# Attention probabilities turned by VectorE block transposes and DMA instead of TensorE transposes

## The reference, cut to what matters

```python
h = x @ w_in[l] + b_in[l]              # q, k, v, z_a, u_g, v_g, z_g, g_a, g_g
scores = q k^T / 8 - slope * dist      # 8 heads of 64, 2 key heads, blocks of 128 queries,
                                       # each over its own and the previous block of 128 keys
m = max(scores.max(-1), sink)
p = exp(scores - m);  p = p / (p.sum(-1) + exp(sink - m))
y_a = (p @ v) * silu(z_a)
merged = sigmoid(g_a) * (y_a @ w_branch_attn) + sigmoid(g_g) * (y_g @ w_branch_gmlp)
x = layer_norm(ALPHA * x + merged @ w_out + b_out)
```

## Time and profile before

| | us |
|---|---|
| median of 3 runs | 1548.91 (1548.21 to 1549.33) |
| profiled execution, its own time | 1549.3 |
| its span in the profile | 1547.5 |
| TensorE busy | 1536.1 |
| VectorE busy | 1012.6 |
| ScalarE busy | 593.4 |
| GpSimd busy | 361.9 |

### The profile page before, as it was taken

The page is one execution under the profiler, slowest core; times in us unless marked ns, Lnnn a source line. Parts: engine busy times, 40 slices in busy tenths (PEclk is TensorE's granted clock), DMA queues, the critical chain, the costliest instruction groups (busy, mean ns, idle before and its releaser), DMA issues.

```text
span 1547.5 us, 29869 instructions
## 1 busy us (share of the span) xinstructions
PE 1536.1 (99%) x12455; PEld 1378.0 (89%) x12455; DVE 1012.6 (65%) x1686; ACT 593.4 (38%) x1070; POOL 361.9 (23%) x333
## 2 busy tenths in 40 slices
PE   9999999999999999999999999999999999999998
PEld 9999999999998899899998898888888988888887
DVE  6656565775867678586786676567516776576346
ACT  5323232253444344334444446482112346641121
POOL 0000000020422224042242124334530043343510
PEclk9999999999999999999999999999999999999999
DMA  5322322323342423424234143223224322222331
GB/s 170 110 82 89 103 83 82 110 82 109 91 131 78 117 91 111 118 76 124 85 98 152 55 135 101 73 72 102 89 82 149 117 83 82 82 82 82 117 128 55
DMA packets 130226, 153.97 MB, mean 99 GB/s; under 512 B 5196, under 2 KB 104944, under 8 KB 130096
## 3 DMA queue, kind: packets, MB, share of 16 engines
q1 hardware_dynamic: 119728, 138.71, 29.2%
q10 hardware_dynamic: 10288, 13.18, 2.5%
q0 software_dynamic: 80, 0.20, 0.1%
HBM read 143.43 MB, written 8.65 MB: 98 GB/s over the span
## 4 chain that ended last, share of the span: by engine, by line
PE 51%; DVE 1%; issue 0%
PE acc L410 14%; PE acc L412 14%; PE acc L411 14%; PE aux L412 1%; PE aux L411 1%; PE aux L410 1%; PE aux L1410 1%; PE aux L1440 1%; PE aux L1429 1%; PE aux L1430 0%; PE aux L1464 0%; PE aux L1377 0%; PE aux L638 0%; PE aux L640 0%; PE aux L571 0%; PE acc L1328 0%
## 5 line engine op out<-in xcount | busy, mean ns | idle before, releaser
L410 PE MATMUL acc<-xhis,whi 128*128 128x264 f32 (+2 forms) x1848 | 610.9, 331 | 0.0
L412 PE MATMUL acc<-xhis,wlo 128*128 128x264 f32 (+2 forms) x1848 | 602.2, 326 | 0.0
L411 PE MATMUL acc<-xlos,whi 128*128 128x264 f32 (+2 forms) x1848 | 601.8, 326 | 0.0
L412 PEld LDWEIGHTS acc<-xhis,wlo 128*128 128x128 f32 x1848 | 347.8, 188 | 29.3
L410 PEld LDWEIGHTS acc<-xhis,whi 128*128 128x128 f32 x1848 | 348.0, 188 | 28.9 <-issue 0.3
L411 PEld LDWEIGHTS acc<-xlos,whi 128*128 128x128 f32 x1848 | 348.2, 188 | 27.0
L405 POOL TENSOR_TENSOR wlo<-raw,whi 128x1024 fp32r<-128x1024 f32 x84 | 207.8, 2475 | 376.9 <-DVE whi L2591 376.9
L401 ACT ACTIVATE whi<-raw 128x1024 fp32r<-128x1024 f32 x158 | 164.0, 1048 | 132.4 <-PE acc L412 119.3
L405 DVE TENSOR_TENSOR wlo<-raw,whi 128x1024 fp32r<-128x1024 f32 x81 | 99.8, 1236 | 38.0 <-ACT whi L401 37.8
L2286 DVE TENSOR_TENSOR wlo<-raw,whi 128x1024 fp32r<-128x1024 f32 x77 | 95.0, 1236 | 27.3 <-ACT whi L401 27.1
L2591 DVE CAST whi<-raw 128x1024 fp32r<-128x1024 f32 x84 | 66.8, 797 | 54.0 <-PE acc L412 53.8
(11 more groups left out here) (392 smaller groups left out, 2784.8 us busy)
## 6 DMA issues: line engine op xcount, KB each, us to landing
raw<-in_w_in SPq DMA_DIRECT2D x38, 1024.0 KB, 5.3
raw<-in_hgrn_w_in SPq DMA_DIRECT2D x32, 1024.0 KB, 5.8
raw<-in_pool_w_in SPq DMA_DIRECT2D x15, 1024.0 KB, 5.6
raw<-in_pool_w_out SPq DMA_DIRECT2D x8, 1024.0 KB, 5.1
raw<-in_hgrn_w_out SPq DMA_DIRECT2D x8, 1024.0 KB, 5.1
raw<-in_w_out SPq DMA_DIRECT2D x8, 1024.0 KB, 5.1
v_turn<-vb ACTq DMA_DIRECT2D x8, 544.0 KB, 2.7
raw<-in_pool_w_grp SPq DMA_DIRECT2D x4, 1024.0 KB, 5.3
```

Source lines behind the costliest of these rows:

```text
L410: pe.matmul(dst, stat[0], mov[0], start=first, stop=False)
L411: pe.matmul(dst, stat[0], mov[1], start=False, stop=False)
L412: return pe.matmul(dst, stat[1], mov[0], start=False, stop=last)
```

## The change

Each scaled probability tile is transposed in blocks of 32x32 by VectorE (`dve.transpose`, two a step, on the probability of s-1, after the maximum) into one of three tiles `pb`. ScalarE writes the tile to `p_turn` in device memory in step s+2 (one DMA of 256 KB, 2 KB a row) and, for two probabilities at once, reads it back in four DMAs of 128 KB (runs of 512 bytes) into `pt`, which puts the blocks in their places. The reads are issued in the steps of `BACK_AT`. The value products run at the steps of `VALUES_AT` and wait for the reads (`pt_landed`). The transposes on TensorE and the copies on ScalarE are gone. In a step ScalarE issues the reads, then computes exp, then issues the write. Values and spatial weights are turned in step 6. The gated values use one buffer in place of two. The last value products come in step 19, one later than before.

```diff
+        pb = [rows[:, 0:SEQ].rearrange("p (b n j) -> p b n j", b=4, n=4) for rows in (sq[1], xn[1], kf)]
+        VALUES_AT = {10: 0, 14: 1, 17: 2, 19: 3}
+        BACK_AT = {4: 0, 6: 1, 10: 2, 11: 3, 14: 4, 15: 5, 17: 6, 18: 7}
+        p_turn = nc.dram_tensor("p_turn", (32, len(ATT), 4, SEQ), F32).ap()
...
 # att_tensor
-                for t in range(s - 6, s - 2) if s >= 6 and s % 4 == 2 else ():
+                for t in range(4 * VALUES_AT[s], 4 * VALUES_AT[s] + 4) if s in VALUES_AT else ():
-                    pe.wait_ge(apt_ready, 1 + base + t + 1)
+                    if b == 0:
+                        pe.wait_ge(pt_landed, 32 * (base + t + 4))
-                                           pt[t % 4][:, 2 * x + kb_, :],
+                                           pt[t % 4][:, :, 2 * x + kb_, :],
...
-                    for x in range(2):
-                        for kb_ in range(0 if b else 1, 2):
-                            mm = pe.transpose(aux2[:, 0, P * (2 * x + kb_):P * (2 * x + kb_ + 1)],
-                                              pr[t % 2][:, x, P * kb_:P * kb_ + P], ident[:, :])
...
 # att_scalar
-                    act.wait_ge(apt_full, base + t + 1)
...
-                    act.activation(pt[t % 4][:, :, :].rearrange("p (x k) q -> p x k q", x=2)[:, :, first:, :],
-                                   aux2[:, 0, :].rearrange("p (x k q) -> p x k q", x=2, k=2)[:, :, first:, :],
-                                   ACT.Copy).then_inc(apt_ready, 1)
+                if between is not None:
+                    between()
+                if 2 <= s < len(ATT) + 2:
+                    n = base + s - 2
+                    act.wait_ge(pb_ready, 2 * n + 2)
+                if s in BACK_AT:
+                    t = 2 * BACK_AT[s]
+                    for n in (base + t, base + t + 1):
+                        act.wait_ge(pb_sent[n % 3], 16 * (n // 3) + 16)
...
+                    if base + t >= 4:
+                        act.wait_ge(ao_full, base + 4 * (t // 4))
+                    for b in range(4):
+                        act.dma_start(pt_pairs[t // 2 % 2][32 * b:32 * b + 32, :, :, :, :].rearrange("p t a n j -> p (t a) (n j)"),
+                                      p_turn[:, t:t + 2, :, P * b:P * b + P].rearrange("p t a n -> p (t a) n")).then_inc(pt_landed, 16)
                 if s < len(ATT):
...
+                if 2 <= s < len(ATT) + 2:
+                    n = base + s - 2
+                    act.dma_start(p_turn[:, s - 2, :, :].rearrange("p a n -> a p n"),
+                                  pb[n % 3].rearrange("p b n j -> p (b n j)")).then_inc(pb_sent[n % 3], 16)
...
 # att_vector, behind the maximum of s
+                if 1 <= s < len(ATT) + 1:
+                    t = s - 1
+                    first, z = (0 if ATT[t][1] else 1), t % 2
+                    dve.wait_ge(aprob, 3 * (base + t) + 3)
+                    n = base + t
+                    if n >= 3:
+                        dve.wait_ge(pb_sent[n % 3], 16 * (n // 3))
+                    for x in range(2):
+                        dve.transpose(pb[n % 3][:, :, 2 * x + first:2 * x + 2, :].rearrange("p b k j -> p k b j"),
+                                      pr[z][:, x, P * first:2 * P].rearrange("p (k b j) -> p k b j", b=4, j=32))\
+                           .then_inc(pb_ready, 1)
```

More of the change, by code:

```diff
@@ L270, in program @@
                 brow = sb("brow", [P, D], where=in_rows)
-            pt_more = [sb(f"pt{s}", [P, 4, P], where=before_g) for s in (2, 3)]
+            pt_second = sb("pt_second", [P, 2, 4, 4, 32], where=before_g)
         gac = sb("gac", [P, 4, SEQ], where=in_c)
@@ L290, in program @@
             pr = [sb(f"pr{s}", [P, 2, 2 * P + 1], where=before_m) for s in range(2)]
-            pt = [sb(f"pt{s}", [P, 4, P], where=before_m) for s in range(2)] + pt_more
+            pt_first = sb("pt_first", [P, 2, 4, 4, 32], where=before_m)
+            pt_pairs = [pt_first, pt_second]
+            pt = [pt_pairs[t // 2][:, t % 2, :, :, :] for t in range(4)]
             sgc = [xn[0][:, 0:SEQ], rstd[:, 0:SEQ]]
@@ L355, in program @@
         aexp, aprob, sink_ready = sem("aexp"), sem("aprob"), sem("sink_ready")
-        apt_full, apt_ready, ao_full = sem("apt_full"), sem("apt_ready"), sem("ao_full")
+        pb_ready, pb_sent = sem("pb_ready"), [sem(f"pb_sent{n}") for n in range(3)]
+        pt_landed = sem("pt_landed")
+        ao_full = sem("ao_full")
         ya_ready, yahi_ready, yalo_ready = sem("ya_ready"), sem("yahi_ready"), sem("yalo_ready")
@@ L865, in c_slots @@
                     if stage == "za" and index == 0:
-                        side.append(("vtc", 0))
-                        side.append(("ws", 0))
+                        pass
                     elif att < len(ATT) and stage in ("za", "u", "vg", "zg", "ga", "gg"):
                         side.append(("att", att))
+                        if att == 6:
+                            side += [("vtc", 0), ("ws", 0)]
                         att += 1
-                    elif att < len(ATT) + 3 and att >= len(ATT):
+                    elif att <= max(VALUES_AT) and att >= len(ATT):
                         side.append(("att", att))
@@ L1419, in att_tensor @@
                         pe.wait_ge(kc_low, 4 * i + 4)
-                        pe.wait_ge(ws_ready, i + 1)
                     if b == 0:
@@ L1431, in att_tensor @@
                     mm.then_inc(asc_full, 1)
[L1432 to L1437, removed]
-                    for x in range(2):
-                        for kb_ in range(0 if b else 1, 2):
-                            mm = pe.transpose(aux2[:, 0, P * (2 * x + kb_):P * (2 * x + kb_ + 1)],
-                                              pr[t % 2][:, x, P * kb_:P * kb_ + P], ident[:, :])
-                    mm.then_inc(apt_full, 1)
             def side_tensor(i, what, n):
@@ L1455, in side_tensor @@
                 elif what == "att":
-                    if n == 0:
+                    if n == min(VALUES_AT):
                         pe.wait_ge(vtc_ready, i + 1)
+                        pe.wait_ge(ws_ready, i + 1)
                     att_tensor(i, n)
@@ L1589, in _ @@
         def _(act):
-            act.sem_inc(apt_ready, 1)
             act.sem_inc(on_ready, 1)
@@ L1871, in att_scalar @@
                 base = 16 * i
+                if between is not None:
+                    between()
                 if 2 <= s < len(ATT) + 2:
-                    t = s - 2
-                    z, first = t % 2, (0 if ATT[t][1] else 1)
-                    act.wait_ge(apt_full, base + t + 1)
-                    if t >= 4:
-                        act.wait_ge(ao_full, base + t - 3)
+                    n = base + s - 2
[4 more added lines that the diff above has]
+                        act.wait_ge(pb_sent[n % 3], 16 * (n // 3) + 16)
                     if t == 2:
                         act.wait_ge(res_ready, 4 * i + 4)
-                    act.activation(pt[t % 4][:, :, :].rearrange("p (x k) q -> p x k q", x=2)[:, :, first:, :],
-                                   aux2[:, 0, :].rearrange("p (x k q) -> p x k q", x=2, k=2)[:, :, first:, :],
-                                   ACT.Copy).then_inc(apt_ready, 1)
-                if between is not None:
-                    between()
+                    if base + t >= 4:
[3 more added lines that the diff above has]
+                                      p_turn[:, t:t + 2, :, P * b:P * b + P].rearrange("p t a n -> p (t a) n")).then_inc(pt_landed, 16)
                 if s < len(ATT):
@@ L1887, in att_scalar @@
                     act.wait_ge(arow, base + s + 1)
+                    if i and s < 2:
+                        act.wait_ge(pb_ready, 2 * (base + s - 1))
                     for x in range(2):
@@ L1891, in att_scalar @@
                            .then_inc(aexp, 1)
-                if s >= 3 and ATT[s - 3][1] == CH - 1:
-                    p = ATT[s - 3][0]
+                if 2 <= s < len(ATT) + 2:
+                    n = base + s - 2
+                    act.dma_start(p_turn[:, s - 2, :, :].rearrange("p a n -> a p n"),
+                                  pb[n % 3].rearrange("p b n j -> p (b n j)")).then_inc(pb_sent[n % 3], 16)
+                if s in VALUES_AT:
+                    p = VALUES_AT[s]
                     act.wait_ge(ya_ready, 1 + 4 * i + p + 1)
-                    act.activation(yah[:, p, :], sq[p % 2][:, 0:SEQ], ACT.Copy).then_inc(yahi_ready, 1)
+                    act.activation(yah[:, p, :], sq[0][:, 0:SEQ], ACT.Copy).then_inc(yahi_ready, 1)
             for i in range(DEPTH):
@@ L2513, in att_vector @@
                     if b < 2:
+                        if s == 0:
+                            dve.wait_ge(c_landed, 32)
+                            dve.wait_ge(lc_landed, 96 * i + 96)
                         dve.tensor_copy(sc[z][:, :, 2 * P:2 * P + 1], sinks[:, 2 * p:2 * p + 2].unsqueeze(2))\
@@ L2523, in att_vector @@
```

(17 more changed lines are left out.)

## The result

The changed kernel is slower: 1565.66 us median (1564.73 to 1566.97, 4 runs) against 1548.81 (1548.21 to 1549.33, 4 runs), a ratio of 1.0108 with a 95% interval of 1.0096 to 1.0120. The forecast was 1541, the range 1535.5 to 1548, and the chance given to slower 0.10. Both forecast and range were wrong.

What follows compares the result with a forecast made beforehand. TensorE was taken as the bound, busy 1536.1 of 1547.5 us. Removed transposes -12.3, ScalarE's ring +1.0 and waits for turned probabilities +3.0 gave -8.3 us, a forecast of 1541, range 1535.5 to 1548.

Steps and rivals of the forecast that it cites:

- Removed transposes: TensorE, attention steps: 112 transposes gone, four cost 0.44 us and two 0.22 by score-product spacing, 12.3 us saved.
- Moving operand in runs of 32: TensorE's value products: reading probabilities as four runs of 32 columns per row brings no cost, nor gain.
- VectorE's block transposes: VectorE, after the maximum: 64 added, some 0.7 us a step and 20 us in all, hidden, cost 0.
- DMA issues: ScalarE's queue: 32 writes at 0.4 us and 64 reads at 0.37 us, 0.63 as the reads' other end.
- Rival (c): ScalarE's queue held by DMA issues averaging 1.0 us beside weight loads: +10.7 us, 1560; chance 0.10.
- The ring in zg: ScalarE's sigmoid-to-sigmoid turn, steps 11 to 14: 6.03 to 6.43 us; TensorE waits 0.5 a layer, +1.0 in all.
- The new wait: TensorE waits for turned probabilities before value products, chiefly at step 19: 1.5 us a layer, +3.0 in all.
- the wait at step 19: TensorE before the last value products, waiting for reads issued in step 18: 0 to 3.2 us.
- TensorE idling before a weight piece: Sign of a wrong mechanism: TensorE idles most elsewhere than forecast, such as step 10 or 14 or a weight piece.
- rival (a): All added work hidden: reads meet no weight load and ScalarE's ring keeps its slack; -12.3 us, 1537; chance 0.27.

Runs made afterwards that it cites:

- e4: The kernel before without 104 of its 112 probability transposes on TensorE, so the value products read what the buffers hold; 1537.45 us.
- e6: The changed kernel with only p_turn's dimension order altered, so a write is 128 rows instead of 4 blocks of 32 rows; 1538.64 us.
- e7: The changed kernel with p_turn laid out for writes of 128 rows and each write issued first in its step; 1537.81 us.
- e1: The changed kernel with its last value products at step 21 instead of 19 and the last two probabilities in their own tile; 1551.91 us.
- e5: The changed kernel with each step's write issued at its start, ahead of reads and exp, instead of behind exp; 1542.19 us.

## Why the prediction was wrong, point by point

- **Removed transposes, -12.3**: right. e4 gives 0.11 us each, and the spacing of steps 1 to 4 is the predicted one.
- **Moving operand in runs of 32, and VectorE's block transposes, 0 each**: right. At full clock the value products take 1.68 us a batch of 28 as before (e6: 1057.16 to 1058.84). A pair of block transposes takes 0.76 us against the 0.7 taken, and e7, which has all 64 of them, is within 0.4 us of e4, which has none.
- **DMA issues**: reads 309 to 1262 ns with a median of 472, between the 0.37 and 0.63 given; writes 527 against the 0.4 taken. Rival (c), slower by issues beside a weight load that average 1.0, was right in its direction alone: a few issues are that long, their average is not.
- **The ring in zg**: TensorE waits 0.8 us a layer at step 15 where 0.5 was taken (bounds 0 to 1.9). The size is near, the reason was wrong, and so this hit is luck. The write behind exp was to lengthen the ring by 0.4, to 6.43. It lengthens nothing: it is issued while exp runs, and in step 12 exp to the next sigmoid takes 3.72 us (1023.25 to 1026.97) against 3.71 before (1024.22 to 1027.93). The ring through step 11, with its four reads, stays at 6.03 (1012.37 to 1018.40). What lengthens it in the steps after that is in the last section.
- **The new wait**: this step failed, in its first term: "A write of 256 KB lands in 2.2 us". That was o_turn's row, a DMA of the same size but another shape. The new one has 4 blocks as its slowest dimension in memory, keeps a quarter of the DMA engines busy, and holds up its reads for 6.7 us or more. With 8.4 from the write of step 17, the last reads start 4.6 us after the eviction that I took to set them, and the reads land 4.4 after their issue (4.2 to 4.5): the wait at step 19 was 5.8 a layer, outside the 0 to 3.2 I gave, and not 1.5.
- **A term that was missing**: ScalarE itself waits for a write ahead of the reads of steps 4 and 6, and exp and the gelus stand behind them. I had worked out where each read lands, but not what stands behind the wait for the write. With a write that lands in 2.0 to 2.3 us this term is nothing, as e6 shows; at 6.7 the stop in step 4 is 3.0 and 3.3 us on TensorE in the two layers. TensorE idling before a weight piece was one of the prediction's own signs that its mechanism is wrong.
- **TensorE's clock behind a wait**: priced at nothing. It was some 8 us in all, on 17.9 us of long waits.

With its one wrong duration put right the kernel lands in the range: e6 takes 1538.64, between the forecast of 1541 and rival (a)'s 1537. The terms are then -12.3, 1.6 for the ring where 1.0 was taken, and no wait at step 19 where 3.0 was: -10.7, and -10.0 measured. The last reads of e6 land 2.6 us after their issue, so at step 19 rival (a) was nearer than the forecast.

## What to carry to other kernels

The price of a DMA can't be taken from a row of equal size alone: write down the dimensions of both sides, slowest first, and take the row of one whose slowest dimension is spread alike; where there is none, the price has a bound of several times the row (here 2.2 us by the row, 6.7 and more in the kernel). Then ask of each wait that a change puts into an in-order queue what stands behind it there, not only whether its own data come in time. And where TensorE may idle for several us, add what it loses afterwards at 1.2 GHz: some 8 us on 17.9 of waits here, though behind one wait of 3.4 us in e1 it lost nothing.

## What the runs showed that was not expected

In the steps that have no reads, two waits now precede exp (for the block transposes, then for the maximum), and its table load moved behind the second. ScalarE before, in the changed kernel, and with the write first, each in step 12:

```profile
1022.26 1.28 ACT L1889 ACT_TABLE_LOAD   x1
1024.22 0.41 ACT L1889 ACTIVATE pr<-sc,sm 128x129 f32<-128x129 f32 x1 [0.68 <-DVE sm L2523]
```

```profile
1021.96 1.28 ACT L1892 ACT_TABLE_LOAD   x1 [2.87 <-DVE sm L2533]
1023.25 0.41 ACT L1892 ACTIVATE pr<-sc,sm 128x129 f32<-128x129 f32 x1
```

```profile
1015.02 1.28 ACT L1894 ACT_TABLE_LOAD   x1
1017.84 0.41 ACT L1894 ACTIVATE pr<-sc,sm 128x129 f32<-128x129 f32 x1 [1.53 <-DVE sm L2531]
```

Before, and in e7, the table load lies beside VectorE's work and only exp waits. In the changed kernel the load of 1.28 us waits too, and so it is in the ring: the sigmoids of this turn are 8.57 us apart (1018.40 to 1026.97) against 6.86 before (1021.07 to 1027.93) and 7.24 in e7 (1014.31 to 1021.55). e7's 0.38 more than before is VectorE's: its statistics, pushed back by the block transposes, end at 1015.51, so it starts on the sigmoid's result 1.11 us after the sigmoid's start (1015.42) where before it was 0.72 (1021.79). The changed kernel has the same 1.11 (1019.51); its other 1.33 is the load. Both e6 and the changed kernel, with the write behind exp, have the load in the ring and TensorE's 0.8 us at step 15; e7 and e5 have neither. In e7, where the write's own wait stands ahead, exp is left with one wait. That it is the number of waits that moves the load is read from the code beside these rows; no run changed that alone.
